# First attention: gates and softmax sums applied to the product with the values, once per head pair and branch, instead of to each softmax

## The reference, cut to what matters

```python
def block(qb):
    ...
    p_cmp = masked_softmax(sc, cmp_end[None, :] <= t[:, None])
    o_cmp = jnp.einsum('bgrqn,bngd->bqgrd', p_cmp, vc.astype(jnp.float32))
    ...
    p_sel = masked_softmax(ss, (pos_sel <= t[None, None, :, None])[:, :, None])
    o_sel = jnp.einsum('bgrqk,bgqkd->bqgrd', p_sel, v_sel.astype(jnp.float32))
    ...
    p_win = masked_softmax(sw, win_mask)
    o_win = jnp.einsum('bgrqk,bkgd->bqgrd', p_win, v_win.astype(jnp.float32))
    g = lax.dynamic_slice_in_dim(gates, s, Q_BLOCK, 1).reshape(B, Q_BLOCK, G, R, 3)
    o = g[..., 0:1] * o_cmp + g[..., 1:2] * o_sel + g[..., 2:3] * o_win
```

## Time and profile before

| what | us |
|---|---|
| median of 3 runs (lowest, highest) | 1902.99 (1901.24, 1904.53) |
| the profiled execution's own time | 1904.76 |
| span of the profile | 1902.8 |
| TensorE busy in the span | 1874.4 |
| VectorE busy in the span | 1151.3 |
| ScalarE busy in the span | 769.0 |
| GpSimd busy in the span | 270.3 |

### The profile page before, as it was taken

The page is one execution under the profiler, slowest core; times in us unless marked ns, Lnnn a source line. Parts: engine busy times, 40 slices in busy tenths (PEclk is TensorE's granted clock), DMA queues, the critical chain, the costliest instruction groups (busy, mean ns, idle before and its releaser), DMA issues.

```text
span 1902.8 us, 23947 instructions
## 1 busy us (share of the span) xinstructions
PE 1874.4 (99%) x9210; PEld 1493.2 (78%) x9210; DVE 1151.3 (61%) x1858; ACT 769.0 (40%) x1652; POOL 270.3 (14%) x209
## 2 busy tenths in 40 slices
PE   9999899999999999999999999999999999999999
PEld 7886666888888888766678888888777788888887
DVE  7466896755454466588775445445979574445353
ACT  5545665332232233366643223223358543233231
POOL 2000341211010021011121101101211021011010
PEclk9999999999999999999999999999999999999999
DMA  6222000323333323322122333322342133333333
GB/s 227 68 89 67 23 2 1 100 89 100 100 96 93 99 87 102 105 73 78 56 89 93 96 100 100 91 97 85 103 112 62 51 92 96 100 100 92 97 94 94
DMA packets 51392, 166.52 MB, mean 88 GB/s; under 512 B 6864, under 2 KB 7248, under 8 KB 51024
## 3 DMA queue, kind: packets, MB, share of 16 engines
q1 hardware_dynamic: 51280, 165.00, 28.3%
HBM read 155.01 MB, written 2.10 MB: 83 GB/s over the span
## 4 chain that ended last, share of the span: by engine, by line
PE 91%; DVE 7%; ACT 1%; issue 1%; DMA 1%; POOL 0%; SPq 0%; DVEq 0%; ACTq 0%
PE bank L925 25%; PE bank L927 25%; PE bank L926 25%; PE bank L1035 2%; PE bank L1091 2%; PE bank L899 2%; PE bank L901 2%; PE bank L900 2%; PE bank L948 1%; PE bank L1126 1%; PE bank L1063 1%; DVE WL L1516 1%; PE bank L1139 1%; DVE PB L1765 1%; DVE SM L1733 1%
## 5 line engine op out<-in xcount | busy, mean ns | idle before, releaser
L1226 ACT ACTIVATE WH<-RAW 128x512 fp32r<-128x512 f32 (+2 forms) x584 | 331.8, 613 | 730.8 <-PE bank L927 667.8
L1516 DVE TENSOR_TENSOR WL<-RAW,WH 128x512 fp32r<-128x512 f32 (+2 forms) x584 | 460.8, 824 | 63.4 <-ACT WH L1226 56.9
L925 PE MATMUL bank<-GH,WH 128*128 128x512 f32 x1088 | 435.6, 400 | 0.0
L925 PE MATMUL bank<-HH,WH 128*128 128x512 f32 x1056 | 425.2, 403 | 2.7 <-DVE HL L1531 1.9
L927 PE MATMUL bank<-GH,WL 128*128 128x512 f32 x1088 | 425.0, 391 | 0.0
L926 PE MATMUL bank<-GL,WH 128*128 128x512 f32 x1088 | 424.6, 390 | 0.0
L927 PE MATMUL bank<-HH,WL 128*128 128x512 f32 x1056 | 413.2, 391 | 0.0
L926 PE MATMUL bank<-HL,WH 128*128 128x512 f32 x1056 | 413.0, 391 | 0.0
L925 PEld LDWEIGHTS bank<-GH,WH 128*128 128x128 f32 x1088 | 205.0, 188 | 44.4 <-issue 3.7
L2034 POOL TENSOR_TENSOR TMP<-TMP,RST 128x512 f32<-128x512 f32 x66 | 116.8, 1769 | 864.4 <-DVE TMP L1951 864.4
L926 PEld LDWEIGHTS bank<-GL,WH 128*128 128x128 f32 x1088 | 205.1, 189 | 43.1 <-issue 3.2
(11 more groups left out here) (238 smaller groups left out, 1892.4 us busy)
## 6 DMA issues: line engine op xcount, KB each, us to landing
RAW<-in_wgu SPq DMA_DIRECT2D x132, 512.0 KB, 3.5
RAW<-in_wd SPq DMA_DIRECT2D x48, 512.0 KB, 3.5
RAW<-in_wd SPq DMA_DIRECT2D x24, 384.0 KB, 3.1
RAW<-in_da_qk SPq DMA_DIRECT2D x16, 512.0 KB, 3.5
TMP<-TMP SPq DMA_DIRECT2D x104, 64.0 KB, 2.0
RAW<-in_w_inh SPq DMA_DIRECT2D x12, 512.0 KB, 3.5
RAW<-in_w_out SPq DMA_DIRECT2D x8, 512.0 KB, 3.5
RAW<-in_da_v SPq DMA_DIRECT2D x8, 512.0 KB, 3.5
```

The costliest lines, as they stand in the source:

```text
L925: e.matmul(b, w_h, hi[st.x][k], start=(k == 0), stop=False)
L1226: e.activation(whs[s % NW][:, a:b], raw[s % NR][:, a:b], ACT.Copy).then_inc(S["wh"], 1)
L1516: e.tensor_tensor(wls[s % NR][:, a:b], raw[s % NR][:, a:b], whs[s % NW][:, a:b].bitcast(F), ALU.subtract).then_inc(S["wl"], 1)
```

## The change

The 32 steps `wt` of first attention are gone, and transposes start from the bare exponents. A head pair and branch is 8 softmaxes; there are 8 of these groups, numbered `kb`. The product with the values of one group now stands alone in bank 7 and is scaled afterwards:

- `nsc` (DVE): after the group's 8 exponents, one reciprocal of 8 sums and one product with 8 gates, tokens on partitions, 8 columns.
- `nsw` (ACT): spreads the 8 columns to 128x512, each 64 wide.
- `nst` (PE): four transposes of it into bank 6, which makes it a scale in the layout of `ob`.
- `nsx` (ACT): copies that to SBUF. The first transposes of the next group wait for it.
- `nmu` (DVE): bank 7 times the scale, into one of two tiles. The next group's first product with values waits for it.
- `nad` (POOL): adds the tile to `OM`.

The compressed branch no longer starts bank 7. Its four products are steps `cmp` (PE, bank 3) with copies `oc` (ACT) into `OM`, and take the place of the four `nom`. `mixa` of tile k waits for `nad` 2k+1.

```diff
@@ plan: softmax, 362 @@
-            o.add("PE", ("tn", a, i), w // 128 * 110, ("wt", a, i if a == "d" else i // 2 * 2), ("tc", *chain[g - 1]) if i else prior)
-            if a == "n" and i % 2:
-                o.add("DVE", ("wt", a, i - 1), 400 + 2 * w, ("ex", a, i), ready(i))
+            before = ("tc", *chain[g - 1]) if i else prior
+            if a == "n" and i and i % 8 == 0:
+                before = ("nsx", i // 8 - 1)
+            o.add("PE", ("tn", a, i), w // 128 * 110, ("wt" if a == "d" else "ex", a, i), before)
...
+    for k in range(4):
+        o.add("PE", ("cmp", k), 900, ("c_va", 1), ("c_tpa", 3), take=("nb", ("oc", k)))
+        o.add("ACT", ("oc", k), 560, ("cmp", k))
...
-            o.add("PE", ("vl", "n", n), w // 128 * 110 + 160 + (900 if n % 16 == 1 else 0), ("tc", "n", n), ("e_vgv", 3),
-                  n % 16 == 1 and (("nom", n // 16 - 1) if n > 1 else ("c_va", 1)))
-        if n % 16 == 15:
-            o.add("ACT", ("nom", n // 16), 500, ("vl", "n", n))
+            o.add("PE", ("vl", "n", n), w // 128 * 110 + 160, ("tc", "n", n), ("e_vgv", 3),
+                  n % 8 == 1 and (("nmu", n // 8 - 1) if n > 1 else ("e_vgv", 3)))
+        if n % 8 == 7:
+            kb = n // 8
+            o.add("DVE", ("nsc", kb), 220, ("ex", "n", n), ("e_vgr", 3))
+            o.add("ACT", ("nsw", kb), 560, ("nsc", kb), ("zerosg",), kb >= 2 and ("nmu", kb - 2))
+            o.add("PE", ("nst", kb), 440, ("nsw", kb), ("tc", "n", n))
+            o.add("ACT", ("nsx", kb), 560, ("nst", kb))
+            o.add("DVE", ("nmu", kb), 720, ("nsx", kb), ("vl", "n", n), kb >= 2 and ("nad", kb - 2))
+            o.add("POOL", ("nad", kb), 1500, ("nmu", kb), ("oc", kb // 2))
...
@@ ScalarE, 1386 @@
-            def nom(k):
-                p.wait_ge(S["vl"], 16 * (k + 1))
-                e.activation(OM[:, k * T:(k + 1) * T], ob, ACT.Copy).then_inc(S["n_om"], 1)
+            def nsw_(kb):
+                p.wait_ge(S["n_sc"], kb + 1)
...
+                e.activation(nsw[kb % 2].rearrange("p (c d) -> p c d", d=64),
+                             NSC[kb % 2].unsqueeze(2).to_broadcast([128, 8, 64]), ACT.Copy).then_inc(S["n_sw"], 1)
+
+            def nsx(kb):
+                p.wait_ge(S["n_st"], kb + 1)
+                e.activation(nsw[kb % 2], ptb, ACT.Copy).then_inc(S["n_sx"], 1)
...
@@ VectorE, 1752 @@
-                    p.then(e.reciprocal(SM[:, o + 2:o + 11:8], SM[:, o + 1:o + 10:8]))
-                    p.settle()
-                    for c in range(2):
...
-                        e.tensor_scalar(q, q, SM[:, o + 8 * c + 2:o + 8 * c + 3], gate, ALU.mult,
-                                        ALU.mult).then_inc(S["nm"], 1)
...
+                p.then(e.reciprocal(rec, sums))
+                p.settle()
+                e.tensor_tensor(to, rec, gates_, ALU.mult).then_inc(S["n_sc"], 1)
+
+            def nmu(kb):
+                p.wait_ge(S["vl"], 8 * (kb + 1))
+                p.wait_ge(S["n_sx"], kb + 1)
+                p.wait_ge(S["n_om"], kb - 1)
+                e.tensor_tensor(nt[kb % 2], ob, nsw[kb % 2], ALU.mult).then_inc(S["n_mu"], 1)
...
@@ GpSimd, 2027 @@
+            def nad(kb):
+                o_ = OM[:, kb // 2 * T:(kb // 2 + 1) * T]
...
+                e.tensor_tensor(o_, o_, nt[kb % 2], ALU.add).then_inc(S["n_om"], 1)
```

More of the change, by code:

```diff
@@ L679, in program @@
         VC = p1(36, T)
+        nt, nsw = [p1(12, T), p1(13, T)], [p1(8, T), p1(9, T)]
+        NSC = [SM[:, 224 + 8 * k:232 + 8 * k] for k in range(4)]
         W2, KC, KCT = P1[:, 37 * T:37 * T + 128], P1[:, 37 * T + 128:37 * T + 192], P1[:, 37 * T + 192:37 * T + 320]
@@ L1092, in tn, with cmp, nst @@
                 done.then_inc(S["tp"], 1)
+            def cmp(k):
+                p.wait_ge(S["c_vc"], 8)
+                p.wait_ge(S["c_pt"], 4)
+                norm_bank("n_oc", k + 1)
+                e.matmul(nb, VC[:, k * 128:(k + 1) * 128], PTC[:, k // 2 * T:(k // 2 + 1) * T],
+                         start=True, stop=True).then_inc(S["n_cm"], 1)
+            def nst(kb):
+                p.wait_ge(S["n_sw"], kb + 1)
+                p.wait_ge(S["tc"], 8 * (kb + 1))
+                for i in range(4):
+                    done = e.transpose(ptb[:, i * 128:(i + 1) * 128], nsw[kb % 2][:, i * 128:(i + 1) * 128], ident)
+                done.then_inc(S["n_st"], 1)
             def vl(a, n):
@@ L1501, in _ @@
                      "c_k1a": c_k1, "c_k2a": c_k2, "c_va": c_v, "c_sma": c_sm, "c_tpa": c_tp, "ex": ex, "tc": tc,
-                     "nom": nom, "omca": omc, "omha": omh, "mixa": mix, "boundsa": bounds, "lama": lam_, "e_ha": e_h,
+                     "oc": oc, "nsw": nsw_, "nsx": nsx, "omca": omc, "omha": omh, "mixa": mix, "boundsa": bounds, "lama": lam_, "e_ha": e_h,
                      "lv0a": lv0, "deca": dec, "wh0a": wh0, "eqea": eqe, "wia": wi, "hsqa": hsq, "hrsa": hrs,
```

63 lines of the change are left out of this document (35 added, 28 removed), and 3 rows, old and new, of tables (PRE, first).

## The result

| | before | after |
|---|---|---|
| median of 20 runs each (lowest, highest), us | 1902.39 (1898.69, 1904.61) | 1904.72 (1902.50, 1906.30) |
| span of the profiled execution, us | 1902.8 | 1902.9 |
| ratio to before, with its 95% interval | | 1.0019 [1.0013, 1.0025] |

A forecast was written before the change was run, and what follows sets the result against it. VectorE was taken to bound 205 to 320 us; its net -21.2 us, +2 for GpSimd, and TensorE's 90 plus 12 lost made 13 us less: 1904.8 to 1891.8, less 1.8 to the median, 1890.0 us (range 1881 to 1899).

The forecast's parts named there:

- VectorE is the bound of 205 to 320 us: Attention beside HGRN: VectorE busy for 107.1 of 115 us, while TensorE needs about 85.
- Taken from VectorE, -27.7 us: In 205 to 320 us: 44 weight multiplications (24.4 us) and 21 double reciprocals (3.3 us) go.
- Added to VectorE, +6.5: In 205 to 320 us: six nsc at 0.4 us and six nmu at 0.69 us.
- GpSimd's additions, +2 for VectorE: Six nad in 205 to 320 us lengthen VectorE's instructions by 2 us, within bounds of nothing and 8.5.
- From need to length, 12 us lost: In 205 to 320 us: TensorE's 90 us plus 12 lost, instead of 8, give 102 of 115.
- The waits that come: First vl waits for nmu, first tn for nsx; chain about 3.3 us per group, mostly costed at nothing.
- named signs of being wrong: Waits over 2 us at nmu or a group's first tn, longer two-input VectorE instructions, or a longer 143 to 205 us.
- The clock, counted as 0: End of attention: low clock in 320 to 325 us counted as 0, with 1.5 us either way.
- Nothing to be seen: Rival: hand-overs of 1.5 to 3 us in six groups cancel the release; 1899 to 1907 us, chance 0.09.
- Slower: Rival: eight uncovered bank 7 hand-overs of 3.3 us outweigh the 21 released; 1908 us, chance 0.07.
- GpSimd gives half of it back: Rival: additions hold VectorE for their full length, or HGRN's halves queue behind them; 1894 to 1898 us, chance 0.17.
- It doesn't do what it says: Rival: another chain, such as HGRN's levels, set the length; time of "Nothing to be seen", no chance of its own.

The follow-up runs named there:

- e6: Kernel before in its own order, first attention's weight multiplications do nothing and nothing replaces them; 8.0 us less, ratio 0.9957 to before.
- e15: Changed kernel in its own order, but nsc, nsw, nst, nsx, nmu and nad do nothing and nobody waits for them; ratio 0.9993 to before.
- e2: Changed kernel with its order and waits, but GpSimd adds only 8 of 512 columns in each nad; ratio 1.0001 to before.
- e8: Changed kernel with the nad additions on VectorE, in the scheduler's plan too; ratio 0.9993 to before.
- e10: Changed kernel with nad on VectorE, scheduler still planning the removed multiplications with their old durations, not executed; ratio 0.9998 to before.
- e11: Changed kernel with nad on GpSimd, scheduler still planning the removed multiplications with their old durations, not executed; ratio 1.0016 to before.
- e19: Plan of e18 kept, but nad is executed by VectorE at its place there; ratio 0.9992 to before.
- e18: Changed kernel with four maxima moved ahead of HGRN's steps at two places and three weight splits back at their old places; ratio 0.9997 to before.
- e7: Kernel before without first attention's weight multiplications, nothing in their place, all engine orders planned anew; 4.3 us less, ratio 0.9977 to before.
- e4: Changed kernel with three VectorE weight splits moved back to their places before the change; ratio 0.9994 to before.
- e12: Kernel before with three weight splits moved forward, between HGRN's first differences and first merge; ratio 1.0016 to before.
- e3: Changed kernel with the scale made for one query block only: 128 of 512 columns, one transpose instead of four; ratio 1.0016 to before.
- e16: Like e15, but nmu runs with another tile as scale and bank 7 is handed over again; ratio 0.9980 to before.

## Why the prediction was wrong, step by step

- *VectorE is the bound of 205 to 320 us.* Half right. Its load shares in the length (e6: 8.0 us less), but a share of 95% of the time busy was no measure of it.
- *Taken from VectorE, -27.7 us.* The count was right (25.7 in the ruler's stretch); **this is the step that failed**: it was booked in full, as if the rest of VectorE's work would keep its length. Without any added step 10.8 us come back in e6 and 9.8 in e15: instructions that now run beside GpSimd take longer, 8.6 us of it in three groups with two inputs. Rows 4 and 5 had the sign, for they say that part of the multiplications' own time was GpSimd's. And the 0.15 to 0.2 us that the prediction read there as what a met instruction loses is an average over met and unmet ones: on line 1888 it is 0.41 us alone and up to 0.96 beside GpSimd.
- *Added to VectorE, +6.5.* Right in sum, by luck: five groups and not six fall in the stretch, and `nsc` takes 0.6 us and not 0.4. `nmu`, `nsc`'s reciprocals and products take 3.4 + 1.0 + 2.1 = 6.5 us.
- *GpSimd's additions, +2 for VectorE.* The term itself is near: e2 takes 2.7 us off VectorE, not the 8.5 of the upper bound. The additions cost 3.4 to 5 us of time (e2, e8, and e10 against e11), but 1 us in e19 against e18. The first two lengthen VectorE's work ahead of HGRN; how much of the time that is, no run shows. Altogether VectorE needs 97.2, where the forecast in the same ruler is 106.1 - 25.7 + 6.5 + 2 = 89.
- *From need to length, 12 us lost.* The second failure. The fullest engine is not TensorE with 90 us, to which the 12 were added, but still VectorE with 97.2, and it is idle for 20.0 us. ScalarE did not come near either (77.4 us in 205 to 320, forecast 85). The 12 fit VectorE in the old order (e6: 12.3); planned anew, the same work has 18.6 (e7). The prediction treated the plan as given, although the diff changes the scheduler's input, and three splits in it are worth 3 to 5 us (e4, e12).
- *The waits that come.* Right as far as costed at nothing: no wait of TensorE for `nmu` or `nsx` is among the long ones, e3 and e16 show their chain hidden. VectorE does wait for the last `vl` ahead of `nmu`, 9.5 us in 4 waits over 143 to 345 us, one of them 4.1 long at 178 us, in TensorE's stretch, and one 4.0 at the tail, where TensorE had `wo` products. Two of the named signs of being wrong showed: such waits over 2 us, which cost nothing that shows, and longer two-input instructions, which did.
- *The clock, counted as 0.* Wrong in size, not settled in amount. See below.
- *The rivals.* "Nothing to be seen" (1899 to 1907 us) has the measured time, but by hand-overs of 1.5 to 3 us that e3 and e16 don't show. "Slower" had the sign but named the wrong place: bank 7 isn't it. "GpSimd gives half of it back" was real in kind, but through HGRN's halves more than through the additions. "It doesn't do what it says" comes nearest in what decides, and got least room. A rival on the scheduler's order was missing.

Summed in the ruler: 8.9 us less work on VectorE and 14.1 us more idle time make the stretch 5.2 longer. The forecast had 17.1 us less work on the fullest engine and 4.1 more idle time, so 8 us of the miss lie in the work and 10 in the idle time. From before to e6 it is -8.5, from e6 to e7 +6.2, and from e15 to after +7.0. These differences mix with a clock that varies by several us from one order to the next, so they don't add up to a us. What holds e8 at 0.9993, with its idle time 5 us above that of before, stays open, as does the part of the lost time that is the clock's alone.

## What to carry to other kernels

An engine that is busy for 95% of a stretch doesn't set its length by that alone: take the operation out in the old order with nothing in its place first, and see what it is worth at most. Where GpSimd works beside VectorE, time taken from VectorE can come back in part as longer instructions: here 10.8 of 25.7 us. And where a scheduler makes the order, a change of its durations is a change of the order: look at what it put ahead of the instructions for which the idle engine waits, above all work that nobody wants yet.
